# A two-layer hybrid backbone on one core: partial sums read by halves, the first softmax ahead of the norm, squares added on VectorE, an opening in another order

## Chip, core and metric

One core of a Trainium2 chip runs the whole program. The metric is the device time of one execution in microseconds (us), the median of three runs. TensorE (PE) multiplies, VectorE (DVE) and ScalarE (ACT) do the elementwise work, SyncE (SP) issues the DMAs of the weights, GpSimd (POOL) does almost nothing.

## What is computed

256 latent and 256 context tokens of width 1024 go through two layers that share their weights between the two streams. Only the first layer updates the context, so layer 0 works on 512 tokens in most places and layer 1 on 256. Per layer:

```python
h = rmsnorm(x) * (1 + scale1) + shift1
proj = h @ w_in                       # 3856 columns: k, v, xbc, dt, C, q, z, hyena
y = concat(ssd(proj), attention(proj), hyena(proj))   # each 512 wide, each with its own rmsnorm
x = x + g1 * (y @ w_out)
h = rmsnorm(x) * (1 + scale2) + shift2
x = x + g2 * ((silu(h @ w_gate) * (h @ w_up)) @ w_down)
```

The SSD is bidirectional with 8 heads, the attention has 8 query and 2 key heads of 64, the hyena part is a long convolution by transforms. The end is one rmsnorm. Everything is float32.

## The kernel before

The program is written by hand, one instruction stream per engine, with semaphores between them. A helper object `p` counts: `p.sig(instruction, name)` raises a semaphore at the instruction's end, `p.after(name, k)` waits for k more, `p.own(name)` waits for all that the engine itself raised, `wait_ge` waits for a total. An engine waits at its next instruction, and whatever stands behind it waits too. Order is what the code says.

Tokens stand along the free dimension: xT holds x as 8 blocks of 128 channels by n tokens (n is 512 or 256). A weight piece is 128 x 1024 numbers. It goes through a ring of four: SP loads it into w_raw, ScalarE rounds it to w_hi (`round_w`, L1281), VectorE makes the remainder w_lo (`split_w`, L1650), TensorE multiplies (L644 to L646, hi by hi, hi by lo and lo by hi) and raises w_used, after which SP may load the piece four further on. So each stage is a loop over pieces, and in it every engine has its `round_w(i+2)` or `split_w(i+2)` at a set place among its other work.

The stages of a layer are in, out, gu0, down0, gu1, down1. What the change touches:

- The opening (layer 0). TensorE sums the squares of x over the channels with a matrix of ones (`stat`, L671), multiplies the conditioning by w_mod (`first_mod_rows`, L568, eight of them, the sums behind the second), makes a filter matmul (L734) and turns the modulation rows (L600, first_mods). ScalarE squares (L1228), takes Ln and Exp (`norm`, rstd), rounds. VectorE computes `argument` (L1706 to L1711, from the filter matmul), xn = xT * rstd in eight instructions (L1724), splits piece 0, reads the modulation (L1668), and then makes hf, and from ScalarE's h_hi the h_lo that TensorE starts on (L688).
- The out stage. Pieces 0 to 7 (`part_half` on TensorE, two half blocks of 128 channels each; `part_residual` on VectorE, L1984) multiply the SSD and then the hyena features, and lie between the steps of the long convolution (`spectrum` L1008, `multiply_spectrum` L1995 to L2001, `convolve` L1020, `hyena_part` L2010) and of the attention. `part_half` of a new piece waits for part_read, the residual of the piece before it, which reads both halves. The attention goes over pairs of heads and tiles: `scores` (L1033), `row_max` (L2020), `softmax` (L1462), `turn_probs` (L1048), `copy_probs`, `attend` (L1067), `divide`. Ahead of it the hyena features' squares are summed (L1109) and turned into hrs (L1475, L1476). Pieces 8 to 11 multiply the attention's features (att_lo, L2109), `residual` (L1687) adds them to x.
- The norm behind out and behind down1 of layer 0. Each chunk of 256 channels has a residual of four instructions (two at n = 256), then ScalarE squares its two blocks (`square_pair`) and TensorE sums each of the eight (`stat`); the norm's table load is L1232, that of Silu behind it L1527.
- FEAT_BANK: PSUM banks into which the four SSD feature blocks are transposed (L702), banks 5, 6, 7 and 5 again. The fourth waits for feat_read, VectorE's f_lo (L1656) of the first.

The order in the out stage on VectorE before:

```python
multiply_spectrum(1, 0)
part_residual(2)
split_w(g0 + 5)
multiply_spectrum(1, 1)
hyena_part(0)
part_residual(3)
hyena_part(1)
```

Of the kernel before, what the change touches and what calls it, by code (L numbers as in the profile page):

```python
# [19 lines left out]
L = 256  # L20
# [68 lines left out]
FEAT_BANK = (5, 6, 7, 5)  # L89
# [6 lines left out]
FIRST_STATS = ((), (0, 1, 2, 3, 4, 5, 6, 7), (), (), (), (), (), ())  # L96
# [101 lines left out]
def backbone(nc, x, c, ctx_in, c_ctx, w_mod, b_mod, norm1_g, w_in, ssd_conv_w, ssd_conv_b, ssd_a_log,  # L198
# [3 lines left out]
    with ExitStack() as stack:  # L202
# [6 lines left out]
        def sem(name):  # L209
# [107 lines left out]
            "eps_ready", "cact_cleared", "decay_rates", "dsel_ready", "mod_rows_copied", "first_mods", "xn_ready", "row_ready", "row_turned", "mods_read",  # L317
            "filt_psum", "spec_ready", "arg_ready", "sine_ready", "taps_read", "taps_ready", "spectra_psum",
            "squares", "square_summed", "rstd_ready", "hf_ready", "h_hi_ready", "h_ready", "dt_psum", "dt_rows", "dt_turned",
# [7 lines left out]
            "att_sq", "att_summed", "att_rms", "att_normed", "att_hi", "att_ready", "part_read",  # L327
# [231 lines left out]
        def _(pe):  # L559
# [112 lines left out]

            def h_pair(g, q, n, between=None):
# [48 lines left out]
            for l in range(DEPTH):  # L722
# [3 lines left out]
                if l == 0:  # L726
                    p.after("cact_ready")
                    for k in range(KD):
                        first_mod_rows(k)
                        for b in FIRST_STATS[k]:  # L730
                            stat(b, T)
                        if k == 1:
                            p.after("sine_ready")
                            p.sig(mm(ps[0:64, 7, L:2 * L], t_w2[0:64, :], t_h[0][0:64, 0, :], start=True, stop=True), "filt_psum")  # L734
                    p.after("mod_rows_copied")
                    p.sig(turn_rows(t_mod, 0, 4), "first_mods")
# [67 lines left out]
                def at_piece(s):  # L804
# [65 lines left out]
                    if s == S_FEAT:  # L870
                        p.after("qkT_ready")
                        p.after("y_normed")
                        p.after("acc_read")
                        to_features(ysum, tiles, FEAT_BANK)

# [103 lines left out]
                def part_half(h):  # L979
# [3 lines left out]
                    if j == 0:  # L983
                        pe.wait_ge(w_lo_done, g0 + i + 1)
                        if i > 0:
                            p.after("part_read")
                        else:
                            pe.wait_ge(pair_free[parts // 2], (q0 - 2) // 2 + 1)
                    last = block_of(g0 + i, parts // 2, j, 4, n, lambda k: mixed(i // 4, k), True, True)
                    if j == 1:  # L990
                        last.then_inc(w_used, 1)

# [137 lines left out]
                p.after("part_read")  # L1130

                for ch in range(4):
# [4 lines left out]
                    for j in range(2):  # L1137
                        last = block_of(i, q0 + ch, j, 4, n, lambda k: mixed(2, k), True, True,
                                        "att_ready" if (ch, j) == (0, 0) else None)
                    last.then_inc(w_used, 1)  # L1140
                    for k in range(max(2 * ch - 2, 0), 2 * ch):
                        stat(k, n)
                stat(6, n)
                stat(7, n)

                for part, (c0, cnt) in enumerate(FFN):
# [21 lines left out]
                    for ch in range(4):  # L1168
                        for sub in range(3):
# [7 lines left out]
                            for j in range(2):  # L1177
                                last = block_of(i, q0 + ch, j, k1 - k0, n, lambda k: (f_hi[:, k0 + k, :], f_lo[:, k0 + k, :]),
                                                sub == 0, sub == 2)
                                if l == 0 and j == 0:  # L1180
                                    mods_in_ffn(ffn_slot(part, 4 * cnt + 3 * ch + sub))
                            last.then_inc(w_used, 1)
                        if part == 1:
                            for k in range(max(2 * ch - 2, 0), 2 * ch):
                                if l == 0:
                                    stat(k, n)
                                else:
                                    turn_final(k)
                    if part == 1 and l == 0:
                        stat(6, n)  # L1190
                        stat(7, n)
# [11 lines left out]
        def _(act):  # L1203
# [20 lines left out]
            def square(k, n):  # L1224

                if k >= 2:
# [3 lines left out]
            def norm(n):  # L1230

                act.preload_act_table_set("natural_log_exp_and_others")  # L1232
                root(n)

            def root(n):

                p.after("square_summed", 2)
# [56 lines left out]
            for l in range(DEPTH):  # L1294
# [4 lines left out]
                if l == 0:  # L1299
# [5 lines left out]
                    norm(T)  # L1305
                    sine(0, 1)
                    round_w(0)
# [17 lines left out]
                for s in range(2, 32):  # L1325
# [119 lines left out]
                    if s == S_FEAT:  # L1445
                        round_features(l, 4, V_SSDG, n, FEAT_BANK)
# [768 lines left out]
```

## Time and profile before

| what | us |
|---|---|
| median of three runs (1366.46 to 1375.18) | 1373.84 |
| the profiled execution | 1373.65 |
| its span | 1371.9 |
| TensorE busy | 1294.2 |
| VectorE busy | 683.6 |
| ScalarE busy | 537.1 |

The span runs from the first to the last instruction. A row of the timeline gives the start in us, the duration in us from the first to the last of the merged instructions, engine, line, operation, output <- inputs, shape and count; in brackets how long the engine had stood before it and what released it. `x4` behind a float32 matmul counts its passes, so two sums over the channels are four.

### The profile page before, as it was taken

The numbers are of one execution on the slowest core, as the hardware profiler recorded it, in microseconds if no ns is written. First come the engines' busy times: TensorE is split into PE (matmuls) and PEld (weight loads), VectorE is DVE, ScalarE is ACT, GpSimd is POOL, SyncE is SP. The second block draws the span as 40 slices with busy tenths as digits, with TensorE's granted clock in tenths as the row PEclk, the third lists the DMA queues.
The fourth block names the chain that finished last, engine by engine and source line by source line (L and its number), as shares of the span: only waits on it lengthen the run. The fifth ranks groups of instructions, "written<-read, shape, count | busy, mean of one in ns | idle before, by whom it ended". The sixth has DMA issues, their size and how long they took to land. (4 is left out here: it accounts for less than half of the span.)

```text
span 1371.9 us, 18208 instructions
## 1 busy us (share of the span) xinstructions
PE 1294.2 (94%) x7636; PEld 1032.3 (75%) x7636; DVE 683.6 (50%) x1146; ACT 537.1 (39%) x912; POOL 2.5 (0%) x8
## 2 busy tenths in 40 slices
PE   5899999999899989999999999989997997999998
PEld 2666777776566767777777788768887766999998
DVE  1653246855566564333322233355478565655553
ACT  4353434542144342222112232256565254444444
POOL 0000000000000000000000000000000000000000
PEclk9999999999999999999999999999999999999999
DMA  9633144341102245445444432313333203465553
GB/s 362 189 123 123 62 139 139 123 138 46 31 17 74 80 121 182 161 147 185 176 172 154 142 95 92 92 46 92 108 108 107 78 16 108 139 185 185 183 174 120
DMA packets 129258, 171.92 MB, mean 125 GB/s; under 512 B 9205, under 2 KB 112279, under 8 KB 128153
## 3 DMA queue, kind: packets, MB, share of 16 engines
q1 hardware_dynamic: 128692, 170.58, 38.5%
q8 instruction: 60, 0.98, 0.3%
q10 hardware_dynamic: 484, 0.18, 0.1%
q14 instruction: 22, 0.17, 0.0%
HBM read 169.69 MB, written 1.05 MB: 124 GB/s over the span
## 5 line engine op out<-in xcount | busy, mean ns | idle before, releaser
L1650 DVE TENSOR_TENSOR w_lo<-w_raw,w_hi 128x1024 fp32r<-128x1024 f32 (+1 forms) x220 | 264.4, 1204 | 307.6 <-ACT w_hi L1281 306.8
L1281 ACT ACTIVATE w_hi<-w_raw 128x1024 fp32r<-128x1024 f32 (+1 forms) x220 | 228.3, 1041 | 395.1 <-DMA w_raw<-in_w_gu_dram 187.6
L644 PE MATMUL ps<-h_hi,w_hi 128*128 128x512 f32 (+1 forms) x896 | 313.1, 349 | 2.5 <-ACT gate L1564 2.1
L645 PE MATMUL ps<-h_lo,w_hi 128*128 128x512 f32 (+1 forms) x896 | 305.4, 341 | 0.0
L646 PE MATMUL ps<-h_hi,w_lo 128*128 128x512 f32 (+1 forms) x896 | 305.3, 341 | 0.0
L644 PE MATMUL ps<-f_hi,w_hi 128*128 128x512 f32 (+1 forms) x544 | 190.1, 349 | 11.3 <-DVE xT L1984 7.2
L644 PEld LDWEIGHTS ps<-h_hi,w_hi 128*128 128x128 f32 x896 | 171.5, 191 | 36.4 <-issue 19.2
L646 PEld LDWEIGHTS ps<-h_hi,w_lo 128*128 128x128 f32 x896 | 171.5, 191 | 19.2
L645 PEld LDWEIGHTS ps<-h_lo,w_hi 128*128 128x128 f32 x896 | 171.6, 192 | 17.1
L646 PE MATMUL ps<-f_hi,w_lo 128*128 128x512 f32 (+1 forms) x544 | 183.7, 338 | 0.0
L645 PE MATMUL ps<-f_lo,w_hi 128*128 128x512 f32 (+1 forms) x416 | 140.1, 337 | 0.0
L644 PEld LDWEIGHTS ps<-f_hi,w_hi 128*128 128x128 f32 x544 | 103.6, 190 | 28.3 <-issue 11.8
L646 PEld LDWEIGHTS ps<-f_hi,w_lo 128*128 128x128 f32 x544 | 103.5, 190 | 11.0
L645 PEld LDWEIGHTS ps<-f_lo,w_hi 128*128 128x128 f32 x416 | 79.0, 190 | 8.7 <-issue 1.0
L688 PE MATMUL ps<-h_hi,w_hi 128*128 128x512 f32 (+1 forms) x128 | 49.5, 387 | 14.1 <-DVE h_lo L1608 6.8
L1687 DVE SCALAR_TENSOR_TENSOR xT<-ps,modv,xT 128x256 f32<-128x256 f32 x72 | 30.4, 478 | 49.6 <-PE ps L646 49.6
L689 PE MATMUL ps<-h_lo,w_hi 128*128 128x512 f32 (+1 forms) x128 | 49.0, 383 | 0.0
L690 PE MATMUL ps<-h_hi,w_lo 128*128 128x512 f32 (+1 forms) x128 | 48.7, 380 | 0.0
L2123 DVE TENSOR_TENSOR hidden<-gate,ps 128x1024 f32<-128x1024 f32 (+1 forms) x22 | 21.0, 953 | 55.0 <-PE ps L646 54.9
L1462 ACT ACTIVATE prob<-ps,sm 128x512 f32<-128x512 f32 (+1 forms) x48 | 29.1, 611 | 46.9 <-DVE sm L2020 46.9
L688 PEld LDWEIGHTS ps<-h_hi,w_hi 128*128 128x128 f32 x128 | 26.1, 204 | 20.2 <-issue 13.9
L1228 ACT ACTIVATE sqr<-xT 128x512 f32<-128x512 f32 (+1 forms) x32 | 17.1, 575 | 61.1 <-PE ps L671 32.9
(291 smaller groups left out, 1678.4 us busy)
## 6 DMA issues: line engine op xcount, KB each, us to landing
w_raw<-in_w_gu_dram SPq DMA_DIRECT2D x88, 512.0 KB, 3.6
w_raw<-in_w_in_dram SPq DMA_DIRECT2D x60, 512.0 KB, 3.9
m_raw<-in_w_mod_dram SPq DMA_DIRECT2D x32, 512.0 KB, 5.0
w_raw<-in_w_down_dram SPq DMA_DIRECT2D x32, 512.0 KB, 3.5
m_even<-in_w_mod_dram SPq DMA_DIRECT2D x12, 1024.0 KB, 5.9
m_odd<-in_w_mod_dram SPq DMA_DIRECT2D x12, 1024.0 KB, 5.9
m_first<-in_w_mod_dram SPq DMA_DIRECT2D x8, 1024.0 KB, 12.1
w_raw<-in_w_out_dram SPq DMA_DIRECT2D x16, 512.0 KB, 3.5
```

The source lines that it names most:

```text
L644: mm(o, w_hi[:, i % RING, w], hi[:, 0:n], start=first and k == 0, stop=False)
L645: mm(o, w_hi[:, i % RING, w], lo[:, 0:n], start=False, stop=False)
L646: last = mm(o, w_lo[:, i % RING, w], hi[:, 0:n], start=False, stop=final and k == nk - 1)
L688: mm(o, w_hi[:, s, w], hi, start=(half == 0 and k == 0), stop=False)
L689: mm(o, w_hi[:, s, w], lo, start=False, stop=False)
L690: last = mm(o, w_lo[:, s, w], hi, start=False, stop=(half == 1 and k == 3))
L1228: p.sig(A(sqr[:, k % 2, 0:n], xT[:, k, 0:n], ACT.Square), "squares")
L1281: A(w_hi[:, i % RING, w], w_raw[:, i % RING, w], ACT.Copy).then_inc(w_hi_done, 1)
L1462: p.sig(A(prob[:, i % 2, j, 0:keys], ps[:, 4 + j, 0:keys], ACT.Exp, bias=sm[:, 0, c:c + 1], accum_out=sm[:, 1, c:c + 1]), "probs_ready")
L1650: TT(w_lo[:, i % RING, w], w_raw[:, i % RING, w], w_hi[:, i % RING, w].bitcast(F32), ALU.subtract).then_inc(w_lo_done, 1)
L1687: ins = STT(out=res, in0=ps[:, 2 * (q % 2) + jj, s * L:(s + 1) * L], scalar=modv[:, l, gate_blk + blk, s:s + 1], in1=res, op0=ALU.mult, op ...
L2123: TT(hidden[:, :, 0:n], gate[:, :, 0:n], ps[:, 2 * ((q + 1) % 2):2 * ((q + 1) % 2) + 2, 0:n], ALU.mult).then_inc(pair_free[(q + 1) % 2], 1)
```

## The change

Six things are done, and nothing else is computed:

- `part_residual` reads half a piece. TensorE raises part_half at the end of the first half, VectorE reads it then; each half block waits only for the residual two halves back. In layer 0 the residuals of halves 4 to 7 stand together behind `hyena_part(0)`. In the attention each half's residual follows one pair after its block. The last two stand around and between the four att_lo.
- `softmax(0)` stands ahead of the wait for hy_summed on ScalarE, and VectorE copies the first pair's probabilities ahead of the four products with hrs.
- Of the eight squares of a norm behind out and down1 (layer 0) six are added by VectorE (`add_squares`, five instructions), and TensorE makes three sums (`stat_rest`) instead of eight.
- The residual of a stage's last chunk is made by halves: tail_half, tail_block.
- `round_w` goes ahead of the squares, and `split_w` ahead of the residual, in the out and down loops.
- The opening: all eight sums and the filter matmul (behind the third) ahead of rows 2 to 7 on TensorE; the second sine ahead of the norm on ScalarE; xn in parts (5, then 1 behind the split, then 2 behind the third hf) on VectorE. In layer 1 the fourth feature block has bank 4.

```diff
-FEAT_BANK = (5, 6, 7, 5)
+FEAT_BANK = ((5, 6, 7, 5), (5, 6, 7, 4))
...
+            def stat_rest(n):
+                p.after("square_added", 5)
+                p.sig(mm(ps[:, STAT, 0:n], ones, lnt[:, 0:n], start=True, stop=False), "square_summed")
+                for k in (KD - 2, KD - 1):
+                    p.after("squares", KD - 1 if k == KD - 2 else 1)
+                    p.sig(mm(ps[:, STAT, 0:n], ones, sqr[:, k % 2, 0:n], start=False, stop=(k == KD - 1)), "square_summed")
...
-                        if i > 0:
-                            p.after("part_read")
-                        else:
-                            pe.wait_ge(pair_free[parts // 2], (q0 - 2) // 2 + 1)
+                    if i > 0:
+                        p.after("part_read")
+                    else:
+                        pe.wait_ge(pair_free[parts // 2], (q0 - 2) // 2 + 1)
...
+                softmax(0)
                 p.after("hy_summed", 4)
                 norm_features(ps[:, other + 1, 0:n], hrs, "hy_rms")
-                softmax(0)
...
                 for ch in range(4):
+                    round_w(g0 + PARTS + ch + 2)
                     if ch > 0:
                         square_pair("out", ch - 1)
-                    round_w(g0 + PARTS + ch + 2)
...
-                    for k in range(KD):
-                        ins = TT(xn[:, k, :], xT[:, k, :], rstd[:], ALU.mult)
-                    p.sig(ins, "xn_ready")
-                    p.own("xn_ready")
+                    scale_x(0, 5)
                     split_w(0)
+                    scale_x(5, 6)
...
                 if l == 0:
                     multiply_spectrum(1, 0)
-                    part_residual(2)
                     split_w(g0 + 5)
                     multiply_spectrum(1, 1)
                     hyena_part(0)
-                    part_residual(3)
+                    for h in range(4, 8):
+                        part_residual(h)
                     hyena_part(1)
...
                 for ch in range(4):
+                    split_w(g0 + PARTS + ch + 2)
+                    if ch >= 2:
+                        add_squares(ch - 2, n)
                     if ch > 0:
                         residual(l, "out", ch - 1, 16, n)
-                    split_w(g0 + PARTS + ch + 2)
+                add_squares(2, n)
                 residual(l, "out", 3, 16, n)
```

VectorE in layer 0's out stage, from the first spectrum product of the second sequence (prod, yspec) to its inverse (yhy), before; xT is a residual, w_lo a split:

```order
L2001 TENSOR_TENSOR yspec<-yspec,prod 128x512
L1984 SCALAR_TENSOR_TENSOR xT<-ps,modv,xT 128x256 x4
L1650 TENSOR_TENSOR w_lo<-w_raw,w_hi 128x1024
L1995 TENSOR_TENSOR prod<-ps,spec 128x512
L1996 TENSOR_TENSOR prod<-ps,spec 128x512
L1997 TENSOR_TENSOR yspec<-ps,spec 128x512
L1998 TENSOR_TENSOR yspec<-ps,spec 128x512
L2000 TENSOR_TENSOR yspec<-yspec,prod 128x512
L2001 TENSOR_TENSOR yspec<-yspec,prod 128x512
L2010 TENSOR_TENSOR yhy<-ps,x_62 128x256 x4
L1984 SCALAR_TENSOR_TENSOR xT<-ps,modv,xT 128x256 x4
L2010 TENSOR_TENSOR yhy<-ps,x_62 128x256 x4
```

And now:

```order
L2037 TENSOR_TENSOR yspec<-yspec,prod 128x512
L1669 TENSOR_TENSOR w_lo<-w_raw,w_hi 128x1024
L2031 TENSOR_TENSOR prod<-ps,spec 128x512
L2032 TENSOR_TENSOR prod<-ps,spec 128x512
L2033 TENSOR_TENSOR yspec<-ps,spec 128x512
L2034 TENSOR_TENSOR yspec<-ps,spec 128x512
L2036 TENSOR_TENSOR yspec<-yspec,prod 128x512
L2037 TENSOR_TENSOR yspec<-yspec,prod 128x512
L2046 TENSOR_TENSOR yhy<-ps,x_62 128x256 x4
L2020 SCALAR_TENSOR_TENSOR xT<-ps,modv,xT 128x256 x8
L2046 TENSOR_TENSOR yhy<-ps,x_62 128x256 x4
```

The residual of halves 4 and 5 has moved from ahead of the second product to behind it and behind the first yhy.

VectorE at the end of layer 1's out stage, before, from the four att_lo to the last residual:

```order
L2109 SCALAR_TENSOR_TENSOR att_lo<-oT,vecT,f_hi 128x256 x4
L1650 TENSOR_TENSOR w_lo<-w_raw,w_hi 128x1024
L1687 SCALAR_TENSOR_TENSOR xT<-ps,modv,xT 128x256 x2
L1650 TENSOR_TENSOR w_lo<-w_raw,w_hi 128x1024
L1687 SCALAR_TENSOR_TENSOR xT<-ps,modv,xT 128x256 x2
L1650 TENSOR_TENSOR w_lo<-w_raw,w_hi 128x1024
L1687 SCALAR_TENSOR_TENSOR xT<-ps,modv,xT 128x256 x2
L1650 TENSOR_TENSOR w_lo<-w_raw,w_hi 128x1024
L1687 SCALAR_TENSOR_TENSOR xT<-ps,modv,xT 128x256 x2
```

And now (lnt is the running sum of the squares):

```order
L2152 SCALAR_TENSOR_TENSOR att_lo<-oT,vecT,f_hi 128x256 x2
L1669 TENSOR_TENSOR w_lo<-w_raw,w_hi 128x1024 x2
L1709 SCALAR_TENSOR_TENSOR xT<-ps,modv,xT 128x256 x2
L1669 TENSOR_TENSOR w_lo<-w_raw,w_hi 128x1024
L1722 TENSOR_TENSOR lnt<-sqr 128x256
L1709 SCALAR_TENSOR_TENSOR xT<-ps,modv,xT 128x256 x2
L1669 TENSOR_TENSOR w_lo<-w_raw,w_hi 128x1024
L1722 TENSOR_TENSOR lnt<-lnt,sqr 128x256 x2
L1709 SCALAR_TENSOR_TENSOR xT<-ps,modv,xT 128x256 x2
L1722 TENSOR_TENSOR lnt<-lnt,sqr 128x256 x2
L1709 SCALAR_TENSOR_TENSOR xT<-ps,modv,xT 128x256 x2
```

Each split now stands ahead of the residual that it followed, and five adds stand in between.

## Rows read from the trace of the kernel before

**Rows 1.** The page: busy us (share of the span) x instructions.

```profile
PE 1294.2 (94%) x7636; PEld 1032.3 (75%) x7636; DVE 683.6 (50%) x1146; ACT 537.1 (39%) x912; POOL 2.5 (0%) x8
```

**Rows 2.** Waits of TensorE: line, waited for: us in total, times, longest.

```profile
PE ps L644 <- DVE xT L1984: 7.2, 5, 1.9
...
PE ps L702 <- DVE f_lo L1656: 4.3, 2, 3.5
PE ps L644 <- DVE att_lo L2109: 4.0, 2, 2.5
PE ps L1033 <- ACT prob L1462: 3.8, 2, 2.1
```

**Rows 3.** Stretches: us, busy of PE, PEld, DVE, ACT, POOL, granted clock, DMA, GB/s.

```profile
42.20:48.90 6.70, 4.68 (x11) 3.75 (x12) 6.55 (x16) 3.35 (x5) 1.04 (x2) 0.50 0.71 178
373.20:383.40 10.20, 9.93 (x42) 6.23 (x42) 6.33 (x13) 3.60 (x10) 0.00 (x0) 0.50 0.00 1
...
1100.40:1103.80 3.40, 3.40 (x12) 2.13 (x10) 3.17 (x8) 1.93 (x5) 0.00 (x0) 0.52 0.00 0
```

**Rows 4.** Timeline of the opening, VectorE and TensorE.

```profile
34.15 4.88 DVE L1724 TENSOR_TENSOR xn<-xT,rstd 128x512 f32<-128x512 f32 x8
...
37.34 1.06 PE L600 MATMUL ps<-c_sq,t_mod 128*128 128x8 f32 x8 [0.72 <-ACT t_mod L1309]
...
40.21 0.25 DVE L1668 TENSOR_TENSOR modv<-ps,vecT 128x16 f32<-128x16 f32 x2
...
44.22 0.76 PE L688 MATMUL ps<-h_hi,w_hi 128*128 128x512 f32 x1 [5.82 <-DVE h_lo L1631]
```

**Rows 5.** Timeline of layer 0's out stage, spectrum products and halves 4 to 7.

```profile
343.64 0.69 DVE L1995 TENSOR_TENSOR prod<-ps,spec 128x512 f32<-128x512 f32 x1 [10.99 <-PE ps L1020]
...
350.92 0.47 PE L644 MATMUL ps<-f_hi,w_hi 128*128 128x512 f32 x1 [1.94 <-DVE xT L1984]
...
351.82 0.69 DVE L1995 TENSOR_TENSOR prod<-ps,spec 128x512 f32<-128x512 f32 x1
...
355.74 1.42 DVE L2010 TENSOR_TENSOR yhy<-ps,x 128x256 f32<-128x256 f32 x4
```

**Rows 6.** Timeline of layer 0, the second pair's scores.

```profile
372.43 2.67 PE L1033 MATMUL ps<-qkT 64*128 64x512 f32 x4 [2.10 <-ACT prob L1462]
```

**Rows 7.** Timelines of layer 0's out stage: first load, last sums, norm.

```profile
459.29 0.37 SPq L404 DMA_DIRECT2D w_raw<-in_w_gu_dram  x1
...
478.95 1.88 PE L671 MATMUL ps<-sqr,c_sq 128*128 128x512 f32 x4
479.15 1.66 DVE L1687 SCALAR_TENSOR_TENSOR xT<-ps,modv,xT 128x256 f32<-128x256 f32 x4 [2.15 <-PE ps L646]
480.84 1.15 ACT L1228 ACTIVATE sqr<-xT 128x512 f32<-128x512 f32 x2 [5.11 <-PE ps L671]
...
482.01 1.28 ACT L1232 ACT_TABLE_LOAD   x1
...
483.55 0.69 ACT L1238 ACTIVATE lnt<-ps,eps 128x512 f32<-128x512 f32 x1 [0.26 <-PE ps L671]
```

**Rows 8.** Layer 1's out stage, timeline; the last row: DMA issues, us to landing.

```profile
1152.49 1.23 DVE L1650 TENSOR_TENSOR w_lo<-w_raw,w_hi 128x1024 fp32r<-128x1024 f32 x1 [1.74 <-ACT w_hi L1281]
...
1154.54 0.72 ACT L1228 ACTIVATE sqr<-xT 128x256 f32<-128x256 f32 x2 [2.08 <-DVE xT L1687]
...
1156.24 1.23 DVE L1650 TENSOR_TENSOR w_lo<-w_raw,w_hi 128x1024 fp32r<-128x1024 f32 x1 [1.74 <-ACT w_hi L1281]
...
1162.04 0.72 ACT L1228 ACTIVATE sqr<-xT 128x256 f32<-128x256 f32 x2 [2.08 <-DVE xT L1687]
...
w_raw<-in_w_gu_dram SPq DMA_DIRECT2D x88, 512.0 KB, 3.6
```

**Rows 9.** Timeline of layer 1's feature blocks and what follows.

```profile
1059.43 1.26 DVE L1656 SCALAR_TENSOR_TENSOR f_lo<-ps,vecT,f_hi 128x256 fp32r<-128x256 f32 x3
...
1064.30 1.04 PE L998 MATMUL ps<-c_sq,hyv 128*128 128x128 f32 x8
```

More of the change, by code:

```diff
@@ L991, in part_half @@
                         last.then_inc(w_used, 1)
+                    else:
+                        p.sig(last, "part_half")
                 def turn_vx(t):
@@ L1624, in normed, with scale_x @@
                     rest(KD - 1)
+            def scale_x(k0, k1):
+                for k in range(k0, k1):
+                    p.link(TT(xn[:, k, :], xT[:, k, :], rstd[:], ALU.mult))
+                p.settle()
             def first_normed(k0, k1):
@@ L1688, in residual, with add_squares @@
                                   scalar=modv[:, l, gate_blk + blk, s:s + 1], in1=res, op0=ALU.mult, op1=ALU.add)
+                    if (ch, jj) == (3, 0) and stage != "down0":
+                        p.sig(ins, "tail_block")
                 ins.then_inc(pair_free[q % 2], 1)
+            def add_squares(ch, n):
+                for k in (2 * ch, 2 * ch + 1):
+                    unread = 0 if k > 0 else 2 if "square_added" in p.made else KD
+                    p.after("squares", unread + 1)
+                    if k > 0:
+                        first = sqr[:, 0, 0:n] if k == 1 else lnt[:, 0:n]
+                        p.sig(TT(lnt[:, 0:n], first, sqr[:, k % 2, 0:n], ALU.add), "square_added")
+                        p.own("square_added")
             p.sig(V.memset(eps1[:, 0:1], EPS), "eps_ready")
@@ L2070, in _ @@
                     hyena_part(0)
[L2071 to L2072 removed]
+                    for h in range(4, 8):
+                        part_residual(h)
                 row_max(0)
@@ L2176, in _ @@
                             hidden_full(part, cnt - 1)
-                        elif s % 3 == 0:
-                            residual(l, f"down{part}", s // 3 - 1, 40, n)
                         split_w(g0 + s + 2)
@@ L2181, in _ @@
                             hidden_low(cnt - 1)
+                        elif s % 3 == 0:
+                            if l == 0 and part == 1 and s >= 6:
+                                add_squares(s // 3 - 2, n)
+                            residual(l, f"down{part}", s // 3 - 1, 40, n)
+                    if l == 0 and part == 1:
+                        add_squares(2, n)
                     residual(l, f"down{part}", 3, 40, n)
```

131 lines of the change are left out of this document (74 added, 57 removed).

## The prediction

> **What bounds the kernel now.** I read the page's busy times first. TensorE is busy for 1294.2 of the span's 1371.9 us [rows 1], so the end is set by its instructions plus some 78 us in which it stands. Then its waits by line: 7.2 us in five waits for the residual DVE L1984, 4.3 us for f_lo in the feature transposes, 4.0 us for att_lo and 3.8 us for the exponentials ahead of the next scores [rows 2]. Third, the granted clock: it falls to one half (1.2 of 2.4 GHz) after TensorE has stood, and in such a stretch each us of work costs another half [rows 3]. Last, the timeline around each edit: the opening [rows 4], the partial sums of layer 0 [rows 5], its first scores [rows 6], the norm behind its output projection [rows 7] and that of layer 1 [rows 8]. The profiled execution took 1373.65 us, 0.19 below the median of the three runs, and 1.75 of it lie outside the span. I work against it.
>
> **Opening.** Before, VectorE computes the second filter argument late, then eight products xn (4.88 us, 0.61 each) from 34.15, then the split of w (1.2), and reads the modulation at 40.21, while the transposed rows of L600 are there from 37.34 + 1.06 = 38.4 [rows 4]. Now six products and the split stand there: from 34.15 that is 3.7 + 1.2, to 39.05, a gain of 1.1 at least. The filter matmul also goes behind the third sum of squares, so the argument no longer holds xn back, only rstd does; one us earlier is enough (38.1) for the start to follow the transposed rows: 40.21 - 38.5 = 1.7 at most, since the rows' own matmuls stay behind all eight sums. A sine and its table load go from behind rstd to ahead of it, which costs ScalarE's chain some tenths and ends in the same bound. The two products moved behind the third hf (1.2) are hidden: each h block keeps TensorE for 12 matmuls. I take **-1.7.**
>
> **Partial sums by halves.** A half block's residual now runs beside the other half. Of the 7.2 us of waits the longest, 1.94, is in layer 0 at 350.92 [rows 5]; the other four, 5.3 us, are in layer 1 and have nothing else behind them except the last (0.9, where the split ahead of it on VectorE keeps half). **-4.8.**
> Layer 0 is different, and this is the place that speaks against the change. VectorE's order is written out: the residual of halves 4 and 5 stood between the two spectrum products and now stands behind both and behind hyena_part(0). TensorE wants it before half 6. After the inverse transform VectorE starts at 343.64 [rows 5]: product 3.8 (its twin runs from 351.82 to 355.7), split 1.2 [rows 8], product 3.8, hyena 1.42, one half residual 0.83 (a quarter of rows 7's 1.66 is one instruction, a half has two). That is 343.64 + 11.1 = 354.8 or 354.9, where the wait before ended at 350.92: half 6 starts 4.0 later. Behind halves 6 and 7 the old wait for yhy, 0.7, is gone. **+3.2**, and TensorE stands some 5.9 us there instead of 1.94.
>
> **First softmax ahead of the norm.** ScalarE sends the two exponentials before it waits for the sum. In layer 0 the scores stood 2.10 us behind them [rows 6]; in layer 1 1.7 (3.8 less 2.1, rows 2). Now they run while TensorE makes the four sums, and hrs is computed as early as before. **-3.8**, with a floor of nothing if the row maxima are later than the sums.
>
> **Last chunks, squares, norms.** Each of the three norms loses five of eight sums on TensorE. Two sums take 1.88 [rows 7], 0.94 each at 512 columns, about half at 256. What follows depends on the chain ScalarE round, VectorE split, adds, residual, ScalarE squares, next round: rounds and splits now stand ahead of squares and residuals, and the adds are new. The trace has no add of this kind; the nearest is xn, 0.61 at 512 columns [rows 4]. Bounds for one add are 0.5 to 0.8 at 512 and 0.3 (half of xn) to 0.6 at 256, where I take 0.7 and 0.45 with its own wait.
> *Norm of layer 1's out stage.* Cycle before: 1156.24 - 1152.49 = 3.75, and the last squares end at 1162.04 + 0.72 = 1162.76 [rows 8]. Counting back three cycles and one residual with its squares, block 0 ended at 1149.8. Now the first load of the next stage is waited for ahead of the residual of block 1: 1149.8 + 3.6 to land [rows 8] + 1.0 + 1.15 + 0.45 + 0.8 + 0.75 = 1157.55; one cycle with two adds, 4.65, gives 1162.2; add 0.5, two half residuals 0.9, one square 0.4 give 1164.0. The sums saved on TensorE are lost in that chain: **+1.3.**
> *Layer 0's out stage.* The same chain: the first load is asked for at 459.3 [rows 7] and lands at 462.9; 5.75 to the squares of block 1, 6.4 for the next cycle, then 0.9, 0.85, 0.85 and 0.6: 478.3. The table load of 1.28 is now uncovered: 479.6, where Ln started at 483.55 [rows 7]. I take **-3.8.**
> *Layer 0's second norm (down1).* Blocks are two and a half times as long, so the chain is hidden. Four sums go ahead of the last block's end, 3.8. Behind it Ln started 4.6 later (483.55 - 478.95, the same shape); now one half residual 0.83, one square 0.6 and the load 1.28 with three handovers make 3.0. **-5.4.** In the last stage the final sums on TensorE hide the earlier halves: 0; a cover gone would cost under 0.5.
>
> The Trainium skill speaks against these norms (ScalarE: Activation LUTs, What ACT_TABLE_LOAD costs): it adds a drain of about 1.38 us to each load of 1.28. The loads lie open in three norms now, so by the page the sum would be 4 us smaller. The trace does not agree: the load of rows 7 ends at 483.29 and Ln starts 0.26 later, when the sums came. I go by the trace.
>
> **Features of layer 1, att_lo.** A fourth bank ends the wait of 3.5 us [rows 2] for f_lo. TensorE then reaches the wait for the fourth f_lo: the first three took 1.26 from 1059.43, so the fourth ends at about 1061.1, and the transposes of hyv went at 1064.30 [rows 9]: **-3.1**. In layer 0 the first att_lo stood behind a whole residual; now a half stands there and a half in the middle: of 2.5 us [rows 2] I take **-1.2** (0.3 to 1.9).
>
> **The clock.** Without it the sum is -1.7 - 4.8 + 3.2 - 3.8 + 1.3 - 3.8 - 5.4 - 3.1 - 1.2 = -19.3. Before, the clock was low for 10.2 us from 373.2, right behind the wait of rows 6, and for 3.4 us from 1100.4, behind the one in layer 1 [rows 3]: 5.1 and 1.7 us lost. Both waits go, so I credit two thirds, 4.3. The new stand of 5.9 us resembles the opening's 5.82, behind which TensorE worked 4.7 us at half clock [rows 4, 3], 2.4 us lost: I charge 2.2. **-2.1.** Both ends: +2.4 if no low stretch goes, -7 if all go and none comes.
> The Trainium skill (TensorE: Matmul & The Clock Gate, HAM oscillation) ties a fall of the clock to gaps longer than these waits. By that rule the two low stretches had another cause and stay, and the sum would be 4 us smaller. The trace shows both right behind the waits, but the same half-filled score matmuls are there too, so I keep a third for the rule.
>
> Sum -21.4: 1373.65 - 21.4 = 1352.
>
> **Rivals.**
> 1. The low stretches stay and the new one comes: -19.3 + 2.4 = -17, 1357 us. For it: the page's rule, and dense part blocks never dropped. Against: the place of both falls.
> 2. The halves and the early softmax don't do what they say, since VectorE or the row maxima are late in the attention loop: -4.8 and -3.8 fall away, 1361 us. Against: a half residual (0.45 in layer 1) beside a block of 12 matmuls is the shorter part, and VectorE's work per pair is unchanged.
> 3. Better: the opening's stand falls from 5.8 to 4.1 us and no low stretch follows it, nor the new one: 1346 us.
> 4. Slower. The stand of 5.9 us drops the clock, and the clock stays down in the attention of layer 0, where a low stretch once lasted 10.2 us although TensorE was busy 9.93 of it [rows 3]. Between rows 6 and rows 7 lie 106 us; each us of them at half clock loses a half. From 39 us of extra low clock on it eats the gain; with 55 it is 1381 us. Against: dense blocks lie between the stand and the attention.
>
> **Numbers.** Forecast 0.64, rival 1 0.18, rival 2 0.08, rival 3 0.06, rival 4 0.04. What a measurement can tell here is about 1%, 13.7 us. Faster by more: nearly all of the forecast, rivals 1 and 3, 0.84; within 1%: 0.12; slower: 0.04. Its own bounds (adds, loads, clock) give 1345 to 1359; with rivals 1 and 2 the range is 1341 to 1363.
>
> **What would show it.** In the new profile: TensorE waits about 5.9 us for a residual near 349 and nothing for residuals in layer 1; the modulation read at 38.5; no wait at the second scores; Ln of layer 1's out norm directly behind its table load and late; 15 sums fewer. Wrong if the stand at 349 is under 3 us (then 1349), if layer 1's out norm gains instead of losing, or if low clock lasts over 60 us in all.

## The result, and the profile after

The changed kernel takes 1351.28 us (median of four runs, 1349.78 to 1351.50), the kernel before in the same comparison 1370.15 us (1365.96 to 1375.18): a ratio of 0.9865, interval 0.983 to 0.9901, so it is faster by 1.35%. The profiled execution took 1351.14 us, span 1349.2; against the profiled one of before that is 22.5 us less. Forecast were 1352.0 us and 21.4 less.

The page of the changed kernel, busy us (share of the span) x instructions; it answers to [rows 1]:

```profile
PE 1278.9 (95%) x7606; PEld 1022.1 (76%) x7606; DVE 691.3 (51%) x1161; ACT 536.8 (40%) x911; POOL 1.8 (0%) x8
```

TensorE works 15.3 us less and stands 7.4 us less (70.3 instead of 77.7). Its waits by line, us in total, times, longest, answer to [rows 2]:

```profile
PE ps L643 <- DVE xT L2020: 6.5, 2, 6.0
PE ps L695 <- DVE h_lo L1621: 6.4, 2, 3.5
...
PE ps L675 <- DVE lnt L1722: 3.2, 2, 2.8
PE ps L643 <- DVE att_lo L2152: 2.7, 3, 1.3
...
PE ps L1009 <- DVE f_lo L1675: 1.6, 1, 1.6
PE ps L643 <- DVE xT L1709: 1.6, 2, 1.1
PE ps L1044 <- ACT prob L1469: 1.5, 3, 0.6
```

Five waits for partial residuals have become two, and of those one is long: the stand of 6.0 us that the forecast named. The fourth f_lo (3.5 us) costs 1.6 at the next line. Two rows are new: the wait for the added squares (lnt) and that for a residual of the last chunks, xT L1709.

Stretches (columns as in [rows 3]). The third and the fifth are the two attentions, where the clock was low before and is full now; in the other three it is low:

```profile
38.00:45.50 7.50, 3.82 (x10) 3.05 (x11) 7.32 (x18) 2.21 (x4) 0.82 (x2) 0.54 0.46 111
348.60:355.40 6.80, 3.17 (x8) 2.52 (x9) 4.17 (x10) 0.00 (x0) 0.00 (x0) 0.53 0.09 31
373.20:383.40 10.20, 9.23 (x74) 5.89 (x72) 8.86 (x18) 6.94 (x17) 0.00 (x0) 1.00 0.00 1
1137.00:1148.00 11.00, 6.31 (x22) 4.97 (x23) 6.34 (x14) 8.01 (x14) 0.00 (x0) 0.53 0.12 41
1082.00:1086.00 4.00, 4.00 (x36) 2.64 (x34) 3.53 (x9) 2.49 (x7) 0.00 (x0) 1.00 0.00 0
```

The opening, and layer 0's out stage around the second spectrum product, answer to [rows 4, 5]:

```profile
36.68 1.06 PE L599 MATMUL ps<-c_sq,t_mod 128*128 128x8 f32 x8 [0.72 <-ACT t_mod L1316]
...
37.85 0.26 DVE L1687 TENSOR_TENSOR modv<-ps,vecT 128x16 f32<-128x16 f32 x2 [0.39 <-PE ps L599]
...
41.68 0.76 PE L695 MATMUL ps<-h_hi,w_hi 128*128 128x512 f32 x1 [3.94 <-DVE h_lo L1650]
```

```profile
349.89 1.42 DVE L2046 TENSOR_TENSOR yhy<-ps,x 128x256 f32<-128x256 f32 x4
...
352.23 0.76 PE L643 MATMUL ps<-f_hi,w_hi 128*128 128x512 f32 x1 [5.96 <-DVE xT L2020]
```

Layer 0's first scores and the ends of its two norms, [rows 6, 7]:

```profile
370.12 0.67 ACT L1469 ACTIVATE prob<-ps,sm 128x512 f32<-128x512 f32 x1
...
372.34 1.13 PE L1044 MATMUL ps<-qkT 64*128 64x512 f32 x4
372.44 0.69 ACT L1482 ACTIVATE hrs<-ps,eps 128x512 f32<-128x512 f32 x1 [0.90 <-PE ps L1120]
...
375.07 1.79 PE L1044 MATMUL ps<-qkT 64*128 64x512 f32 x4 [0.57 <-ACT prob L1469]
...
473.09 1.28 ACT L1243 ACT_TABLE_LOAD   x1
474.38 0.69 ACT L1245 ACTIVATE lnt<-ps,eps 128x512 f32<-128x512 f32 x1
...
874.55 1.23 DVE L1669 TENSOR_TENSOR w_lo<-w_raw,w_hi 128x1024 fp32r<-128x1024 f32 x1 [3.85 <-ACT w_hi L1288]
875.70 1.41 DVE L1722 TENSOR_TENSOR lnt<-lnt,sqr 128x512 f32<-128x512 f32 x2
877.14 1.66 DVE L1709 SCALAR_TENSOR_TENSOR xT<-ps,modv,xT 128x256 f32<-128x256 f32 x4
```

And the end of layer 1's out stage, [rows 8]:

```profile
1124.77 1.06 ACT L1288 ACTIVATE w_hi<-w_raw 128x1024 fp32r<-128x1024 f32 x1 [3.86 <-DMA w_raw<-in_w_out_dram]
...
1125.86 1.23 DVE L1669 TENSOR_TENSOR w_lo<-w_raw,w_hi 128x1024 fp32r<-128x1024 f32 x1 [2.22 <-ACT w_hi L1288]
1127.01 0.87 DVE L1709 SCALAR_TENSOR_TENSOR xT<-ps,modv,xT 128x256 f32<-128x256 f32 x2
...
1134.97 0.88 DVE L1722 TENSOR_TENSOR lnt<-lnt,sqr 128x256 f32<-128x256 f32 x2
...
1138.18 1.22 PE L675 MATMUL ps<-lnt,c_sq 128*128 128x256 f32 x2 [2.84 <-DVE lnt L1722]
...
1139.51 1.28 ACT L1243 ACT_TABLE_LOAD   x1
1141.26 0.47 ACT L1245 ACTIVATE lnt<-ps,eps 128x256 f32<-128x256 f32 x1 [0.47 <-PE ps L678]
```

The same TensorE instructions looked up in both timelines cut the 22.7 us of span into places. The forecast's column has its clock term set where it would act (+2.2 behind the stand, -3.3 and -1.0 in the two attentions):

| from the last place to | before | after | gained | forecast |
|---|---|---|---|---|
| first matmul of in, layer 0 | 44.22 | 41.68 | -2.5 | -1.7 |
| half 6 | 350.92 | 352.23 | +3.9 | +4.0 |
| sums of the hyena squares | 366.62 | 368.70 | +0.8 | +1.4 |
| third attend (L1067, now L1078) | 388.77 | 385.23 | -5.6 | -5.4 |
| first att_lo | 452.16 | 447.64 | -1.0 | -1.2 |
| first matmul of gu0 | 488.24 | 479.08 | -4.6 | -3.8 |
| filter transforms behind down1 | 896.21 | 882.21 | -4.8 | -5.4 |
| inverse transform of layer 1 | 1079.49 | 1062.36 | -3.1 | -3.1 |
| first att_lo of layer 1 | 1146.68 | 1121.08 | -8.5 | -7.5 |
| first matmul of gu0, layer 1 | 1167.54 | 1144.73 | +2.8 | +1.3 |
| end of the span | 1371.9 | 1349.2 | +0.1 | 0 |

### The profile page after: what moved, and what is told of

It is laid out like the page before. It is cut to its first block and busy times, and to the rows that moved or that the text cites. A ratio compares the mean times of both kernels' runs of the same rounds, so it can differ in the third digit from the quotient of the medians.

```text
span 1349.2 us, 18196 instructions
## 1 busy us (share of the span) xinstructions
PE 1278.9 (95%) x7606; PEld 1022.1 (76%) x7606; DVE 691.3 (51%) x1161; ACT 536.8 (40%) x911; POOL 1.8 (0%) x8
## 5 line engine op out<-in xcount | busy, mean ns | idle before, releaser
L957 PE MATMUL ps<-w_hi,h_hi 128*128 128x512 f32 x96 | 40.5, 422 | 0.0
L1420 ACT ACTIVATE em<-ps,bia 128x128 f32<-128x128 f32 x96 | 26.4, 377 | 28.6 <-PE ps L797 28.5
```

The source lines that it names most:

```text
L957: mm(o, h_hi[:, b, tok], w_hi[:, (i + half) % RING, w], start=(b == 0), stop=False)
L1420: ins = A(em[:, 2 * (h % 2) + d, t * P:(t + 1) * P], ps[:, 6 + d, t * P:(t + 1) * P], ACT.Exp, bias=bia[:, t, d * 8 + h:d * 8 + h + 1])
```

## Experiments

All start from the changed kernel. Medians are set against 1351.5 us, that of its eight runs in two comparisons (1349.78 to 1354.44). Since runs of one kernel lie up to 7 us apart (those of the kernel before up to 11.7, 1367.06 to 1378.77), I read each edit in the trace too, as the distance between two TensorE instructions around it.

**The changed kernel again.**

> The changed kernel once more, nothing altered, beside the next three on one chip, since the profiled executions so far differ among themselves: TensorE's transposed modulation rows come at 36.7 to 39.6 us, and the low clock stretches near 160, 480 and 507 are there in some and not in others. Theory: median within 1 us of 1351.3, and each timed run within 3 us of it. Rival: the spread of the same kernel is wider (to 1357), and then the two undone edits measured at 1357.1 and 1357.0 (softmax, bank) say less than they seem to.

Measured: 1352.85 us (1351.26 to 1354.44); its ratio, 0.9851 (0.9816 to 0.9886), repeats the first. The profiled one took 3.05 us longer than the first profile, and 2.3 of that are there already at L599 (38.99 instead of 36.68). Where they come from stands in the last section. So the median holds, and single executions are good to 3 us only.

**Residuals of halves 4 and 5 between the products again.**

```diff
                     multiply_spectrum(1, 0)
+                    part_residual(4)
+                    part_residual(5)
                     split_w(g0 + 5)
                     multiply_spectrum(1, 1)
                     hyena_part(0)
-                    for h in range(4, 8):
-                        part_residual(h)
+                    part_residual(6)
+                    part_residual(7)
```

> The changed kernel, but in layer 0 the residuals of halves 4 and 5 stand between the two spectrum products again; everything else stays as changed. Theory: the moved residual alone makes the stand of 5.96 us at 352.23, and the low clock behind it (3.8 us of work at half clock, 1.9 lost) comes from that stand. Then half 6 starts 4.0 us earlier, TensorE stands about 2 us there, no low stretch follows, and the time is 1351.3 - 4.0 - 1.9 = about 1345.4 us. Rival A: the 4.0 us come back behind it, since the second inverse transform or the first exponentials wait for VectorE anyway: 1349 to 1351. Rival B: the low clock is not tied to the stand and stays: 1347.3.

Measured: 1346.24 us (1344.48 to 1347.80), 5.3 less, ratio to the kernel before 0.9822 (0.9779 to 0.9865). TensorE's wait in its timeline, and its clock where the stand and the low stretch had been:

```profile
356.20 4.12 PE L1031 MATMUL ps<-c_inv,yspec 128*128 128x256 f32 x18 [2.00 <-DVE yhy L2046]
```

```profile
344.00:352.00 8.00, 8.00 (x37) 6.60 (x36) 7.27 (x14) 0.00 (x0) 0.00 (x0) 1.00 0.20 66
```

TensorE works all the 8 us at full clock; 2.0 us of waiting remain, one line later, for yhy. From the forward transform (L1019) to the sums of the hyena squares it takes 48.6 us, 54.3 in the changed kernel: 5.7. Of these 4.0 are the wait (5.96 less 2.00) and 1.7 the clock. The theory holds, and the timeline speaks against both rivals: the moved residual alone makes the stand and what the clock loses behind it. All ten profiled executions that have this stand have a low stretch of 6.8 us there, and none of the four without it.

**The first softmax behind the norm again, on ScalarE.**

```diff
-                softmax(0)
                 p.after("hy_summed", 4)
                 norm_features(ps[:, other + 1, 0:n], hrs, "hy_rms")
+                softmax(0)
```

> The changed kernel, but on ScalarE softmax(0) stands behind the norm of the hyena features again, in both layers (VectorE's order stays as changed). Theory: the second scores wait again for 2.1 us in layer 0 and 1.7 in layer 1, and the low clock comes back behind both waits (5.1 and 1.7 us lost before), against which two or three new waits of 0.4 to 0.6 go: 1351.3 + 3.9 + 6.8 - 1.5 = about 1360.5 us. Rival A (a fall of the clock has another cause than these waits): only the waits come back, no low stretch near 375 and 1081: 1355. Rival B: the waits do not come back since another order hides them: 1351.

Measured: 1357.14 us (1356.72 to 1360.98), 5.6 more. Both waits are back, as a row of each layer's timeline shows; the clock of the two attentions stands behind them:

```profile
374.02 1.36 PE L1044 MATMUL ps<-qkT 64*128 64x512 f32 x3 [2.11 <-ACT prob L1469]
...
1081.78 1.79 PE L1044 MATMUL ps<-qkT 64*128 64x512 f32 x4 [1.68 <-ACT prob L1469]
```

```profile
374.00:384.40 10.40, 9.42 (x63) 5.37 (x65) 7.68 (x17) 5.73 (x14) 0.00 (x0) 1.00 0.00 1
1083.50:1087.50 4.00, 4.00 (x13) 2.37 (x12) 3.44 (x8) 1.94 (x5) 0.00 (x0) 0.57 0.00 0
```

The waits are shown to come from the order, 2.8 us in layer 0 (from the sums of the hyena squares to the third attend 19.3 instead of 16.5) and 2.6 in layer 1 with its clock (from the inverse transform to the wait at 1116.96 57.2 instead of 54.6). The clock settles nothing in favour of my reason: behind a wait of 2.11 us, the same as in [rows 6], it stays at 1.00 in layer 0, where it had been 0.50 for 10.2 us [rows 3]; in layer 1 it falls.

**Layer 1's fourth feature block in bank 5 again** (`FEAT_BANK = ((5, 6, 7, 5), (5, 6, 7, 5))`).

> The changed kernel, but layer 1's fourth feature block is transposed into bank 5 again, as before. Theory: TensorE waits 3.5 us for f_lo again and 1.6 us at the transposes behind it go: +3.1 us, 1354.4 us, with a low stretch of 3.4 us there as before (1059 to 1063), which costs under 0.3 since TensorE mostly waits in it. Rival: the low stretch costs its half, 1.5 us: 1355.9. Rival B: a later wait takes it up: 1351.3 to 1352.

Measured: 1357.02 us (1353.47 to 1360.62), 5.5 more. From the feature transposes (L709) to the inverse transform it takes 25.3 us instead of 20.8: the 3.1 of the wait (3.46 for f_lo is back) and 1.4 of clock, since here a low stretch of 6.8 us follows with TensorE busy for 6.0 of it. That rival had 1355.9. So 4.5 us are shown; the median's 5.5 comes from runs 7.2 us apart (1353.47 to 1360.62), and the profiled one, the slowest of them, also has a low stretch near 507 and L599 2.1 us late.

**The end of layer 1's out stage as before the change.**

```diff
+                    if l == 1:
+                        for k in range(max(2 * ch - 2, 0), 2 * ch):
+                            stat(k, n)
...
-                    round_w(g0 + PARTS + ch + 2)
+                    if l == 0:
+                        round_w(g0 + PARTS + ch + 2)
                     if ch > 0:
                         square_pair("out", ch - 1)
+                    if l == 1:
+                        round_w(g0 + PARTS + ch + 2)
```

(and on VectorE the residual ahead of the split and no adds.)

> The changed kernel, but layer 1's out stage ends as before the change: TensorE makes all eight sums of squares, no adds on VectorE, squares ahead of the round and residual ahead of the split; only the last chunk by halves stays. Theory: the new order and the adds lose there (from the first att_lo to the first matmul of the next stage 23.65 us after, 20.86 before), so undoing them gives back 2.8 us and perhaps 0.5 of low clock: 1351.3 - 2.8 to 3.3 = about 1348.3 us. Rival: the five sums saved on TensorE outweigh them, and the loss came from the clock of that execution alone: 1351.3 or up to 1353.

Measured: 1349.50 us (1348.90 to 1351.46), 2.0 less. From the first att_lo to gu0 it takes 20.96 us against 23.65, so the undone part gives back 2.7 as expected. The eight traces in which this stage is as changed have 23.2 to 24.9 there, those with it undone 20.9 to 21.0. 0.6 of the 2.7 is lost again by the end of the span; behind the first matmul of gu0 TensorE now works 5.6 us at low clock, 2.9 in the changed kernel, but that this is the cause was not tried.

**Only its order undone, the adds kept.**

```diff
                 for ch in range(4):
-                    split_w(g0 + PARTS + ch + 2)
+                    if l == 0:
+                        split_w(g0 + PARTS + ch + 2)
                     if ch >= 2:
                         add_squares(ch - 2, n)
                     if ch > 0:
                         residual(l, "out", ch - 1, 16, n)
+                    if l == 1:
+                        split_w(g0 + PARTS + ch + 2)
```

(and on ScalarE the squares ahead of the round.)

> The changed kernel, but in layer 1's out stage the old order alone: squares ahead of the round, residual ahead of the split; the adds on VectorE and the three sums stay. From the first att_lo to the first matmul of the next stage it was 23.65 us with both edits and 20.96 with both undone. Theory A (the adds are the price: they stand in the chain round, split, add, residual, squares, 0.45 to 0.9 us a turn, and the old order puts one more round into the last turn): the first squares come 2.7 us earlier and the last at the same time, 23.5 us, 1351 us in all. Theory B (the order is the price, since the residual of the first chunk waits for a weight piece that has not landed): 21 us, 1348.6 in all.

Measured: from the first att_lo to gu0 23.71 us. Theory A: the adds are the price. The row of TensorE's timeline:

```profile
1137.44 1.23 PE L675 MATMUL ps<-lnt,c_sq 128*128 128x256 f32 x2 [4.97 <-DVE lnt L1725]
```

The first residual comes early (3.6 us behind the first att_lo, 5.9 in the changed kernel), and the later turns, with one more round in the last of them, take that up. The profiled execution took 1350.91, the median is 1354.29 us (1350.91 to 1354.84); by the trace it is no slower in this stage, so I put the 2.8 down to the spread, which isn't shown. What would fit: the profiled execution, 2.9 us faster than the next, is one of the four without the low clock near 160 (last section), which alone is worth 3.3.

**The opening as before the change.**

```diff
-                    scale_x(0, 5)
+                    scale_x(0, KD)
                     split_w(0)
-                    scale_x(5, 6)
...
-                    scale_x(6, KD)
```

(and TensorE's and ScalarE's order likewise.)

> The changed kernel with the opening as before: rows and sums in the old order on TensorE, the norm ahead of the second sine on ScalarE, eight xn ahead of the split on VectorE. Theory: the modulation is read 1.7 us later behind the transposed rows (2.9 instead of 1.2 us behind the start of L599), the first matmul of the in stage 1.7 us later: 1353.0 us, plus up to 0.9 if the low clock covers more work. Rival: the loads of w_mod decide when the rows come, and the reordering of VectorE is hidden behind them: 1351.3.

Measured: 1350.72 us (1348.35 to 1355.38), no difference that the median can tell. The timeline of TensorE can:

```profile
37.19 1.06 PE L599 MATMUL ps<-c_sq,t_mod 128*128 128x8 f32 x8 [0.72 <-ACT t_mod L1314]
...
44.08 0.76 PE L695 MATMUL ps<-h_hi,w_hi 128*128 128x512 f32 x1 [5.84 <-DVE h_lo L1648]
```

6.89 us lie between the start of the transposed rows and the first matmul, as before the change (6.88), against 5.0 to 5.2 in all twelve executions with the new opening: 1.7 to 1.9 us.

**The first half of the last residual ahead of the last adds.**

```diff
-                add_squares(2, n)
-                residual(l, "out", 3, 16, n)
+                residual(l, "out", 3, 16, n, (0,))
+                add_squares(2, n)
+                residual(l, "out", 3, 16, n, (1,))
```

(likewise in the down stages.)

> The changed kernel, but the residual of the first half of the last chunk stands ahead of VectorE's last two adds instead of behind them (out of both layers, down1). In the changed kernel the adds (1.42 us) stand ahead of both halves, though the first half has been there for a while. Theory: behind the last block only the second half's residual is left, so the Ln of the norm comes 0.7 us earlier in layer 0's out, about 0.9 in its down1, 0.4 in layer 1: 1351.3 - 2.0 = 1349.3 us. Rival: the sum over the adds (L675) is then the late one and TensorE's three sums end no earlier: 1351.3.

Measured: 1351.28 us (1350.70 to 1351.75). Layer 0's out stage gains 0.8 us (att_lo to gu0 30.7 instead of 31.4). In down1 and layer 1 the stages get no shorter: the sum over the adds waits 1.32 us in down1 (0.09 and 0.53 in the two profiles of the changed kernel) and 2.84 in layer 1, as without the edit. That is the rival.

**Both norms of layer 0 as before the change.** (`stat` for all eight squares, no adds, the old order of rounds and splits; the last chunk by halves stays.)

> The changed kernel, but both norms of layer 0 (behind out and behind down1 of its second part) as before the change: TensorE makes all eight sums of squares, no adds, squares ahead of the round, residual ahead of the split; the last chunk by halves stays. Theory: this takes back the two largest terms, 3.8 + 5.4 = 9.2 us by the forecast, 4.0 + 4.3 = 8.3 us by the trace, less up to 1 us that the halves of the last chunk keep: 1351.3 + 7.3 to 8.3 = about 1359 us. Rival (the sums stood in time in which TensorE waits for weights or for VectorE anyway, and the clock did the rest): less than 4 us, under 1355.

Measured: 1359.67 us (1357.79 to 1361.54), 8.2 more. By the trace att_lo to gu0 takes 34.7 us instead of 31.4, and from the first wait for gate (near 505) to the filter transforms 382.5 instead of 378.9: 3.3 + 3.6 = 6.9. Sums, adds and order together are shown to be the largest gain of the change; which part the order has in it was not tried in layer 0. The first of the two is firm (31.4 to 31.5 in every trace with that stage as changed), the second less so: 378.6 to 379.7, and 380.6 in the bank experiment with its low stretch near 507. The profiled execution is 6.9 us longer in all; what the median has beyond that the trace doesn't show. What the two places gained beyond them (1.4 and 0.7 us against before) stays when they go.

**Whole pieces in layer 1 again.**

```diff
                     if i > 0:
-                        p.after("part_read")
+                        if l == 0 or j == 0:
+                            p.after("part_read")
```

(and on VectorE one residual of both halves behind the second.)

> The changed kernel, but in layer 1 the residuals of the partial sums read whole pieces again, behind the second half, and TensorE waits for them once a piece. Theory: the four waits come back (1.06, 1.66, 1.66 and 0.9 us) and with them 5.3 us: about 1356.6 us. Rival: only the two long waits in the attention come back, since new short waits for the exponentials in front of them take up the rest: 3.3 us, 1354.6.

Measured: 1357.01 us (1356.30 to 1358.65), 5.5 more. The four waits are back to the hundredth (1.06, 1.66, 1.66, 0.90); from the inverse transform to att_lo 64.6 us instead of 58.7, of which 0.4 are att_lo's.

**Three edits together.**

> Three of the edits tried singly, put together on the changed kernel: layer 0's residuals of halves 4 and 5 between the spectrum products again, layer 1's out stage ending as before the change, and in layer 0's out stage the first half of the last residual ahead of the last adds. If they add up by the traces (5.7, 2.7 and 0.8 us): 1351.3 - 9.2 = about 1342.1 us, ratio to the kernel before 0.980. Rival: TensorE's clock gives part of it back elsewhere, since the low stretch behind layer 1's norm grew when that norm came earlier (it then covered 6.0 us of work instead of 3.3): 1344 to 1346.

Measured: 1341.00 us (1339.56 to 1342.90), ratio 0.9798 (0.9775 to 0.9822). The parts add up: 9.2 by the traces, 9.4 between the two profiled executions, 10.5 by the medians. It beats both kernels. Of the waits of TensorE for a partial residual only 0.5 us are left:

```profile
PE ps L695 <- DVE h_lo L1631: 6.9, 2, 4.0
PE ps L695 <- DVE h_lo L1660: 3.9, 1, 3.9
PE ps L643 <- DVE att_lo L2165: 2.7, 3, 1.3
PE ps L905 <- DVE st L1942: 2.6, 1, 2.6
PE ps L1031 <- DVE yhy L2057: 2.0, 1, 2.0
...
PE ps L643 <- DVE xT L2031: 0.5, 1, 0.5
```

**And the last adds of down1 ahead of the late split.**

```diff
                             residual(l, f"down{part}", s // 3 - 1, 40, n)
+                        elif (l, part, s) == (0, 1, 10):
+                            add_squares(2, n)
-                    if l == 0 and part == 1:
-                        add_squares(2, n)
```

> The combination measured at 1341.0 us, with one more edit: in layer 0's down1 VectorE's last two adds stand ahead of the split of the last weight piece instead of behind it. In the changed kernel that split waits until 874.55 for a piece that lands late, the adds run from 875.70 to 877.11 behind it, and both halves' residuals only from 877.14, though the first half's block is there some 5 us earlier. Theory (this is what the forecast of 5.4 us for this norm lacked against 4.3 measured): the first half's residual and square are done before the last block ends, and Ln comes 0.8 us earlier, from 503.3 to 882.2 that is 378.9 less 0.8, and 1340.2 us in all. Rival: the last square and its sum decide alone, and nothing moves: 1341.0.

Measured: 1343.11 us (1339.49 to 1345.52), ratio 0.9803 (0.9778 to 0.9828), the same as the combination within the measurement. ScalarE and VectorE in this norm:

```profile
870.35 0.87 DVE L1719 SCALAR_TENSOR_TENSOR xT<-ps,modv,xT 128x256 f32<-128x256 f32 x2
...
873.10 1.28 ACT L1250 ACT_TABLE_LOAD   x1
874.40 0.69 ACT L1252 ACTIVATE lnt<-ps,eps 128x512 f32<-128x512 f32 x1
```

The first half's residual now comes ahead of the sum of adds (871.35), and Ln starts 3.05 us behind that sum, against 3.60 to 3.62 in all ten traces that have the adds and this order. That is the forecast's 3.0. From gu0's gate wait to L775 it is 378.1 us instead of 378.7 in the combination, a difference that lies within what this stretch varies by itself.

## Why the prediction was right, and where its steps were off

The time was right to 0.7 us, and nine of the eleven places of the table lie within 0.8 us of the forecast; the two others, both in layer 1, are off by 1.0 and 1.5 with opposite signs.

**Opening, features, att_lo.** As forecast: the modulation is read 1.2 us behind the start of the transposed rows, the stretch with the fourth f_lo takes 3.07 less, att_lo waits 1.2 less in layer 0. Of the 2.5 us in the opening, 0.7 are none of the change's (L599 itself came 0.66 earlier). And 0.65 is given back near 178, where TensorE now waits 0.69 us for a modulation weight (L577) and waited 0.04 before; the other traces with the new opening have up to 0.48 there. The forecast has no such term.

**The moved residual.** Named at 354.8 with 4.0 us; half 6 starts 4.02 later against what stands ahead of it, the wait is 5.96. Undone alone, 5.7 us with the clock. It is the part of the change that costs, and nothing in what it is for needs it.

**Halves of layer 1.** 4.8 forecast, 5.2 to 5.5 found. I left 0.5 of the last wait standing; it is 0.5. For layer 1's last chunks (L1709) there are two new waits, 0.53 and 1.11 us, where I had written that TensorE waits for no residual in layer 1; they belong to the norm below.

**First softmax.** 3.8 forecast; the second scores start 2.17 and 1.75 us earlier, 3.9 together.

**The clock.** The step that was mis-sized most: -2.1 forecast, about -4.0 found. Less the new waits that came with it, 3.4 are gained in layer 0's attention, 1.1 in layer 1's, 0.7 near 451 and 0.5 in the opening, and 1.7 lost behind the new stand. Of the two stretches behind the scores' waits I had credited two thirds, 4.3 (two thirds of 5.1 + 1.7 would be 4.5). Both went whole, but the full clock uncovers waits of 0.57, 0.39 and 0.57 us for the next exponentials, of which the forecast says nothing: the chain from the scores over row_max and the exponentials seems then longer than what TensorE has in between (not tried). They are no price of the new order, as the softmax experiment has the first two as well (0.57 and 0.39). My reason for the stretches is not borne out either: that experiment has the wait of 2.11 us again without the fall. The Trainium skill (TensorE: Matmul & The Clock Gate, HAM oscillation) ties a fall to longer gaps than these. By that rule, the stand of 6 us agrees (ten of ten), and so does the wait of 2.11 us without a fall; the falls behind 2.10 us in the kernel before and behind 1.68 us in layer 1 do not. What drops the clock in an attention stays open.

**Norm of layer 1's out stage.** The right sign, +1.3 forecast, +2.8 found. The failed step is the start of the chain. I let it begin at the first load of the next stage, as if block 0's residual came on time. It stands behind the split of the last out piece, which is itself rounded only at 1124.77 when it lands, so it starts 2.7 us later than before (5.9 instead of 3.2 behind the first att_lo), block 0's squares come at 1127.91 and the next round behind them. That makes 0.9 at the squares of block 1, the last add 0.2, and at the end Ln waits 0.5 for TensorE's sum at half clock. TensorE, too, waits 0.53 and 1.11 us for the late residuals. By the experiments, adds and order undone give 2.7 back and the order alone nothing, so the price is that of the adds; with the old order the same time goes into a longer chain at the end.

**Norms of layer 0.** Out 3.8 forecast, 4.6 found, with 0.65 of clock; the cycle of 6.4 us is there (6.42). down1 5.4 forecast, 4.3 found. The failed step is "behind it now one half residual": the late split (874.55) and the adds stand ahead of both halves, so Ln comes 3.6 instead of 3.0 us behind the block, and TensorE's gain ahead of it is 3.3, not 3.8. With the adds moved, the 3.0 were measured.

**Table loads.** The Trainium skill (ScalarE: Activation LUTs, What ACT_TABLE_LOAD costs) adds a drain of 1.38 us. In three norms Ln starts 0.01 to 0.5 us behind the load's end (474.38 behind 473.09 + 1.28); in the third case it waits for the sum. The trace has no such drain, and the sum was right to leave it out.

There is luck in the sum: what the two norms lost (+1.5 and +1.1) the clock (-1.9) and the opening's 0.7 made up. And the profiled pair (22.5 us apart) flatters the change against the medians (18.9), as 1373.65 lies above the 1370.15 of its kernel: against the medians the 21.4 of the forecast are 2.5 too many, and the time of 1352 was hit because it was counted from the slower execution.

## What to carry to other kernels

When a residual or a copy is moved, ask first which buffer it frees and who takes that next; here one such move cost 5.7 us in a change that gained 19, and was found in the order alone. Sums handed from a busy engine to an idle one can cost more than they save where blocks are shorter than the chain through the other engines: with 512 columns adds and order gained 3.3 to 3.6 us a norm, with 256 they lost 2.7. And credit a changed clock only where a stand of several microseconds goes or comes; behind waits of 2 us it went both ways.

## What the hardware showed that I had not expected

Low clock comes and goes between executions of identical instructions. Of the fourteen profiled executions, ten have the granted clock at about 0.52 for 6.8 us near 160, in the same matmuls, and four (the softmax, opening, order and whole-piece experiments) do not, though nothing ahead of that place differs except in one (the opening's). The same four also lack a low stretch of 3.4 us near 90 that the other ten have. From the last L795 to the second feature transposes the changed kernel takes 142.2 us, the softmax experiment 138.9. The two windows:

```profile
157.50:164.30 6.80, 6.80 (x30) 6.01 (x30) 2.96 (x4) 2.69 (x9) 0.00 (x0) 0.52 0.00 0
```

```profile
159.00:166.00 7.00, 6.77 (x55) 5.61 (x54) 3.81 (x5) 2.74 (x9) 0.00 (x0) 1.00 0.00 0
```

The first rise of the clock moves as well. The transposes of x come in two groups of sixteen, the first from 14 to 16 on, the second near 19. The second group takes 1.97 us in eight of the fourteen and 3.6 to 3.7 in six. In the first profile of the changed kernel and in its repeat:

```profile
14.65 3.48 PE L726 MATMUL ps<-c_sq,x_nat 128*128 128x128 f32 x16
...
18.64 1.97 PE L726 MATMUL ps<-c_sq,x_nat 128*128 128x128 f32 x16
```

```profile
14.26 3.62 PE L726 MATMUL ps<-c_sq,x_nat 128*128 128x128 f32 x16
...
18.85 3.68 PE L726 MATMUL ps<-c_sq,x_nat 128*128 128x128 f32 x16
```

It is the clock. Its record in a trace begins only with the first stretch at full clock, at 16.6 to 18.7 us in the eight and at 22.1 to 23.8 in the six (17.86 and 23.29 in these two); for the time ahead of it a view of the profile prints 1.00 though there is no record. In all fourteen the transposes ahead of that point start 0.213 us apart, and those behind it, in the eight, 0.109. The transposes of the first attention (L1048, now L1059) do the same under a recorded clock: 0.213 apart in the kernel before at 0.50, 0.109 in the changed one at 1.00. So ahead of the first record TensorE ran at its lower level, and the six executions stay there some 5 us longer. The six are just those in which L599 comes at 38.3 to 39.6 instead of 35.8 to 37.3. Why the rise comes early in one execution and late in another isn't known. The two things, about 2.3 us here and 3.3 near 160, are of the size of the 3 to 7 us by which runs of one kernel differ; that they explain them isn't shown, as only one execution of each run was profiled.
